# Earlier places for five VectorE and ScalarE operations around a block-attention stage

## The reference

```
h = h + moba_mixer(rmsnorm(h, norm_mix), w_qkv, q_gain, k_gain, w_o, rel_bias)
h = h + square(relu(rmsnorm(h, norm_ffn) @ w1)) @ w2

qkv = h @ w_qkv                          # q, k, v: 16 heads of 64
q, k = rmsnorm(q, q_gain), rmsnorm(k, k_gain)   # per head
p = softmax(q k^T / 8 + bias, causal)
o = (p v) @ w_o
```

## Time and profile before

| | us |
|---|---|
| median of 3 runs | 934.1 (933.73 to 934.14) |
| profiled execution, its own time | 932.37 |
| span of the profiled execution | 930.6 |
| DVE busy | 625.5 |
| ACT busy | 488.0 |

### The profile page before, as it was taken

One profiled execution on the slowest core, in us unless ns is written; L12 is line 12 of the kernel. 1 busy time (PEld: TensorE's weight loads), 2 busy tenths in 40 slices (PEclk: granted clock), 3 DMA queues, 4 the chain that ended last, 5 costly groups with the idle time before them and its releaser, 6 DMA issues.

```text
span 930.6 us, 13989 instructions
## 1 busy us (share of the span) xinstructions
PE 904.6 (97%) x5688; PEld 773.1 (83%) x5688; DVE 625.5 (67%) x1079; ACT 488.0 (52%) x732; POOL 38.3 (4%) x66
## 2 busy tenths in 40 slices
PE   9999999999999999988999999999998999999998
PEld 7987788887788887866999988878776799998886
DVE  5469978778888897775766654456677586665441
ACT  6545746646655855463655543346576365554330
POOL 2400010000000001000000000000000000000000
PEclk9999999999999999999999999999999999999999
DMA  8842363642245559550555565556463256655540
GB/s 298 301 145 91 99 202 115 225 135 91 92 148 169 180 200 271 153 146 15 167 183 182 194 207 187 184 179 207 155 204 113 91 181 188 192 196 195 183 157 23
DMA packets 79199, 154.58 MB, mean 166 GB/s; under 512 B 5543, under 2 KB 7879, under 8 KB 79136
## 3 DMA queue, kind: packets, MB, share of 16 engines
q1 hardware_dynamic: 75120, 142.81, 46.6%
q0 software_dynamic: 3872, 10.81, 4.7%
q10 hardware_dynamic: 144, 0.07, 0.0%
HBM read 152.57 MB, written 1.11 MB: 165 GB/s over the span
## 4 chain that ended last, share of the span: by engine, by line
PE 74%; DVE 14%; ACT 8%; issue 3%; DMA 0%; SPq 0%; DVEq 0%; ACTq 0%
PE ps L723 15%; PE ps L725 15%; PE ps L724 15%; PE ps L754 7%; PE ps L755 7%; PE ps L756 7%; DVE w_lo L1826 5%; ACT w_hi L1346 3%; PE ps L1028 1%; DVE area L2172 1%; DVE area L2308 1%; DVE area L2096 1%; ACT y_tok L1477 1%; PE ps_mid L1203 1%; ACT area L1564 1%
## 5 line engine op out<-in xcount | busy, mean ns | idle before, releaser
L1826 DVE TENSOR_TENSOR w_lo<-w_raw,w_hi 128x2048 fp32r<-128x2048 f32 (+1 forms) x134 | 302.3, 2261 | 187.1 <-ACT w_hi L1346 187.0
L1346 ACT ACTIVATE w_hi<-w_raw 128x2048 fp32r<-128x2048 f32 (+1 forms) x134 | 252.9, 1890 | 201.1 <-PE ps L725 147.2
L723 PE MATMUL ps<-w_hi,act_hi 128*128 128x512 f32 (+1 forms) x456 | 182.1, 399 | 2.2 <-ACT area L1364 1.0
L725 PE MATMUL ps<-w_hi,act_lo 128*128 128x512 f32 (+1 forms) x456 | 175.0, 384 | 0.0
L724 PE MATMUL ps<-w_lo,act_hi 128*128 128x512 f32 (+1 forms) x456 | 174.7, 383 | 0.0
L723 PE MATMUL ps<-w_hi,hid 128*128 128x512 f32 x296 | 116.1, 392 | 1.0 <-ACT area L1364 0.5
L725 PE MATMUL ps<-w_hi,hid 128*128 128x512 f32 x296 | 115.3, 389 | 0.0
L724 PE MATMUL ps<-w_lo,hid 128*128 128x512 f32 x296 | 115.2, 389 | 0.0
L754 PE MATMUL ps<-act_hi,w_hi 128*128 128x256 f32 x384 | 110.6, 288 | 0.4 <-DVE act_lo L2018 0.4
L755 PE MATMUL ps<-act_lo,w_hi 128*128 128x256 f32 x384 | 107.5, 280 | 0.0
L756 PE MATMUL ps<-act_hi,w_lo 128*128 128x256 f32 x384 | 107.5, 280 | 0.0
(11 more groups left out here) (356 smaller groups left out, 1231.5 us busy)
## 6 DMA issues: line engine op xcount, KB each, us to landing
w_raw<-in_ffn_w SPq DMA_DIRECT2D x64, 1024.0 KB, 5.3
w_raw<-in_w_in SPq DMA_DIRECT2D x22, 1024.0 KB, 5.5
w_raw<-in_a_w_qkv SPq DMA_DIRECT2D x18, 1024.0 KB, 5.0
w_raw<-in_b_w_qkv SPq DMA_DIRECT2D x12, 1024.0 KB, 5.1
w_raw<-in_w_out SPq DMA_DIRECT2D x8, 1024.0 KB, 5.0
w_raw<-in_b_w_o SPq DMA_DIRECT2D x4, 1024.0 KB, 5.0
w_raw<-in_w_in SPq DMA_DIRECT2D x8, 256.0 KB, 6.2
w_raw<-in_w_in SPq DMA_DIRECT2D x4, 512.0 KB, 3.5
```

The costliest lines, as they stand in the source:

```text
L723: pe.matmul(o, ah, wh, start=first, stop=False)
L725: mm = pe.matmul(o, al, wh, start=False, stop=last)
L1346: act.activation(w_hi[:, c % RING, :, 0:n], w_raw[:, c % RAW, :, 0:n], ACT.Copy).then_inc(w_hi_done, 1)
L1826: dve.tensor_tensor(lo, w_raw[:, c % RAW, :, 0:n], hi.bitcast(F), ALU.subtract).then_inc(w_lo_done, 1)
```

## The change

It moves five things. (1) The norms of heads 8 to 15 are done in two parts: heads 8 and 9 (`block_norms(f + 4, 0, 2)`) where all stood, and the other six in unit 5 behind the staging copy of pair 4; PE waits for the first part before pair 4 and for the second before pair 5. (2) In unit 7 DVE does the staging copy of pair 5 ahead of `scaled(8)` and `scaled(9)`. (3) ACT evicts half 0 of value block `f+5` in unit 8 ahead of the exponentials of units 10 and 11. (4) The split of the weight chunk at `f+6` goes from unit 14 to unit 12 on ACT and to unit 13 on DVE. (5) In `after_half` on DVE, half 0 of a residual block is evicted ahead of the weight split.

```diff
@@ stage_pair, PE
-                if p == 4:
-                    pe.wait_ge(qk_norm, 10)
+                if p in (4, 5):
+                    pe.wait_ge(qk_norm, 10 + 2 * (p - 4))
@@ block_attention, ACT
-                units(3, MOBA_HEADS, {..., 6: lambda: splits(f + 5, 0), 8: lambda: take(f + 5, 0), 9: lambda: splits(f + 5, 1),
-                                       14: lambda: splits(f + 6, 0)},
-                      front={1: lambda: take(f + 3, 1), 9: lambda: take(f + 5, 1)})
+                units(3, MOBA_HEADS, {..., 6: lambda: splits(f + 5, 0), 9: lambda: splits(f + 5, 1),
+                                       12: lambda: splits(f + 6, 0)},
+                      front={1: lambda: take(f + 3, 1), 8: lambda: take(f + 5, 0), 9: lambda: take(f + 5, 1)})
@@ block_norms, DVE
-            def block_norms(b):
+            def block_norms(b, h0=0, n=8):
                 for i in range(2):
-                    at = BLOCKS[b - 1 + i]["c0"]
-                    v = qkv[:, :, at:at + 512].rearrange("p t (h d) -> p t h d", d=HD)
-                    dve.tensor_tensor(v, v, spread(block_st[:, 6, 16 * i:16 * i + 1], [(8, 2), (1, 8), (0, HD)]), ALU.mult).then_inc(qk_norm, 1)
+                    at = BLOCKS[b - 1 + i]["c0"] + HD * h0
+                    v = qkv[:, :, at:at + HD * n].rearrange("p t (h d) -> p t h d", d=HD)
+                    dve.tensor_tensor(v, v, spread(block_st[:, 6, 16 * i + h0:16 * i + h0 + 1], [(8, 2), (1, n), (0, HD)]), ALU.mult).then_inc(qk_norm, 1)
@@ after_half, DVE
                     if also:
                         also()
+                    if BLOCKS[b]["use"] == "residual":
+                        take(b, 0)
                     splits(b, 0)
-                    take(b, 0)
+                    if BLOCKS[b]["use"] != "residual":
+                        take(b, 0)
@@ units, DVE
+                    if ph == 3 and u == 7:
+                        staged(BLOCK_STAGED[u])
                     if ph == 3 and u % 2 and u + 2 < n:
                         scaled(u + 1)
                         scaled(u + 2)
-                    if ph == 3 and u in BLOCK_STAGED:
+                    if ph == 3 and u in BLOCK_STAGED and u != 7:
                         staged(BLOCK_STAGED[u])
@@ block_attention, DVE
                 def hook4():
                     take(f + 4, 1)
-                    block_norms(f + 4)
+                    block_norms(f + 4, 0, 2)
+
+                def hook5():
+                    block_norms(f + 4, 2, 6)
+                    splits(f + 4, 1)
-                units(3, MOBA_HEADS, {..., 4: hook4, 5: lambda: splits(f + 4, 1), 7: ..., 10: ..., 14: lambda: splits(f + 6, 0)})
+                units(3, MOBA_HEADS, {..., 4: hook4, 5: hook5, 7: ..., 10: ..., 13: lambda: splits(f + 6, 0)})
```

More of the change, by code:

```diff
@@ L1629, in hook7 @@
                     splits(f + 4, 1)
-                units(3, MOBA_HEADS, {0: lambda: splits(f + 3, 0), 1: lambda: splits(f + 3, 1), 2: lambda: splits(f + 4, 0), 3: lambda: (take(f + 4, 0), take(f + 4, 1)), 5: lambda: splits(f + 4, 1), 6: lambda: splits(f + 5, 0), 8: lambda: take(f + 5, 0), 9: lambda: splits(f + 5, 1),
-                                       14: lambda: splits(f + 6, 0)},
-                      front={1: lambda: take(f + 3, 1), 9: lambda: take(f + 5, 1)})
+                units(3, MOBA_HEADS, {0: lambda: splits(f + 3, 0), 1: lambda: splits(f + 3, 1), 2: lambda: splits(f + 4, 0), 3: lambda: (take(f + 4, 0), take(f + 4, 1)), 5: lambda: splits(f + 4, 1), 6: lambda: splits(f + 5, 0), 9: lambda: splits(f + 5, 1),
+                                       12: lambda: splits(f + 6, 0)},
+                      front={1: lambda: take(f + 3, 1), 8: lambda: take(f + 5, 0), 9: lambda: take(f + 5, 1)})
                 pair_high(7)
@@ L2246, in hook4 @@
                     take(f + 4, 1)
-                    block_norms(f + 4)
-                units(3, MOBA_HEADS, {1: hook1, 2: lambda: splits(f + 3, 1), 3: lambda: splits(f + 4, 0), 4: hook4, 5: lambda: splits(f + 4, 1), 7: lambda: splits(f + 5, 0), 10: lambda: splits(f + 5, 1), 14: lambda: splits(f + 6, 0)})
+                    block_norms(f + 4, 0, 2)
+                def hook5():
+                    block_norms(f + 4, 2, 6)
+                    splits(f + 4, 1)
+                units(3, MOBA_HEADS, {1: hook1, 2: lambda: splits(f + 3, 1), 3: lambda: splits(f + 4, 0), 4: hook4, 5: hook5, 7: lambda: splits(f + 5, 0), 10: lambda: splits(f + 5, 1), 13: lambda: splits(f + 6, 0)})
                 pair_low(7)
```

## The result

| | before | changed |
|---|---|---|
| median of 4 runs each | 933.91 us | 926.24 us (925.13 to 927.26) |
| ratio, 95% interval | | 0.9925 (0.9907 to 0.9943) |
| profiled execution, own time | 932.37 us | 926.48 us |
| span | 930.6 us | 924.7 us |

The forecast was faster, at 928.7 us with a range from 927.1. Three of the four runs of the kernel before are the ones behind the 934.1 us that the forecast started from.

A forecast was written before the change was run, and what follows sets the result against it. PE was taken to bound the kernel, so only its idle time could be gained: 0.75 + 3.17 + 1.47 = 5.39 us, moving the median from 934.1 to 928.7 us, with a range of 927.1 to 931.0.

The forecast's parts named there:

- Sum: Gains of 0.75 us at moba's entry, 3.17 to pair 4's output and 1.47 at pair 7's output: 5.39 us.
- Entry: At the start of moba, evicting residual half 0 before DVE's weight split removes PE's idle time: 0.75 us.
- Up to the output of pair 4: Mixer lead from norms, staging copy and value eviction together, after a new wait there: 3.17 us.
- Last: Before pair 7's output, PE no longer waits for DVE's copy of unit 15 behind a weight split: 1.47 us.
- lower bound's 4.2 us: Smallest gain: new wait at pair 4 a whole microsecond, first norms at the page's full price; 929.9 us.
- The base: Profiled execution lies 1.7 us under the median, so its forecast 927.0 us becomes a median of 928.7, from 934.1.
- Norms, staging copy: Before pair 4's transposes PE gains 1.60 us, DVE 1.27; before pair 5's scores PE gains 1.53 more.
- Value eviction: At mobao's first step 0.52 us gained, mostly handed back in a 0.45 us wait before pair 4's output.
- Weight split: Split of unit 14 moved into DVE's idle time; pair 6's low part about 1.5 us later, unnoticed; gain 1.47 us.
- second wait: Units 7 to 9: ACT's late half delays pair 5's copy, divisions and split; gain 3.9 us, 930.2; chance 0.15.
- FFN that takes the gain back: Next FFN's start hangs on weight stream or load; mixer's 4.64 us lost, 0.75 left: 933.4 us; chance 0.05.
- lower clock in the mixer: Denser PE work drops TensorE's granted clock to 1.2 GHz; 10 us of it gives 938.7 us; chance 0.02.

The follow-up runs named there:

- e2: Kernel before with only the residual half 0 eviction moved ahead of the weight split; 931.18 us, ratio 0.9991.
- e3: Changed kernel without the residual half 0 eviction ahead of the weight split; 927.75 us, ratio 0.9959.
- e5: Changed kernel with the norms of heads 8 to 15 whole again; 929.01 us in its only execution, a profiled one.
- e6: Changed kernel with DVE's staging copy of pair 5 back behind the divisions of units 8 and 9; 930.18 us in its only execution, a profiled one.
- e11: Changed kernel with DVE's staging copy of pair 5 back behind the divisions of units 8 and 9, run again; median 929.13 us.
- e4: Changed kernel with ACT's eviction of value half 0 back behind the exponentials; median 929.35 us.
- e7: Changed kernel with the weight split back in unit 14; 927.39 us in its only execution, a profiled one.
- e8: Changed kernel with ACT's eviction of value half 1 moved between the exponentials of units 10 and 11; median 927.09 us, ratio 0.9931.
- e12: Same kernel as e8, value half 1 evicted between the exponentials of units 10 and 11; 925.34 us in its only execution, a profiled one.

## Why the prediction was wrong, point by point

- **Sum.** 5.39 us were forecast against the profiled execution; it gained 5.89 (932.37 to 926.48), of which 0.2 us was there before the first place of the change. Entry: 0.75 forecast, 1.05 measured (e2; 1.08 in e3). The step was the choice of idle time over start-to-start distance; the modelled end of the last matmul hides part of a wait, and the first matmul behind a wait is longer. Up to the output of pair 4: 3.17 forecast, 3.02 measured. Last: 1.47 forecast, 1.56 measured. The lower bound's 4.2 us does not follow from its own terms: the wait at a whole microsecond and the full price of the norms make about 4.7.
- **The base: the step that failed.** "It lies 1.7 us under the median, so the median goes from 934.1 to 928.7." The three runs behind 934.1 lay at the upper end of what this kernel does: 42 further runs have medians of 931.54, 932.61 and 932.22 on their three chips. A median of three at its upper end was thus taken for the kernel's time, and the gain of one execution was set against it, while the new time was drawn from the changed kernel's middle. Of the 2.5 us between 928.7 and 926.24 this step is 1.7; the gain of 5.9 instead of 5.4 is 0.5, and the last 0.2 is the distance of the new median from its own profiled execution. Had I set the gain of 5.4 against the profiled execution's 932.37, the forecast would have been 927.0, and 926.24 well within a range as wide. The range took the spread of the three runs, 0.4 us; 930.05 to 936.08 is that of the 42. Why those three lay high isn't known: neither their clocks nor their chip are recorded.
- **Norms, staging copy.** Right in mechanism and size. DVE carried on 1.27 us as forecast (1.26, e5), PE started the scores of pair 5 without a wait. What I did not see is what the old wait can do besides: with the others in, it is 1.9 us long, and in both profiles that have it (e6, e11) the lower clock followed, which makes part 2 worth 2.6 us there.
- **Value eviction.** The new wait before the output of pair 4 came as forecast in place and cause, at 0.9 us instead of 0.45: PE reached mobao 0.3 us earlier than the idle times said, and the output started 0.15 us later. "This part is worth next to nothing, and what it gives is handed back one piece later" was wrong: 1.4 us (e4). I took the part's worth from the wait of the kernel before, 0.52 us, and did not ask how long that wait would be with the other parts in: 2.11 us. The prediction's own numbers had the answer. Without part 3 ACT's chain, 1.60 us earlier, starts mobao at 715.46 - 1.60 = 713.86 and the output at 717.05 - 1.60 = 715.45, against 713.88 with it: 1.57 us. The sum was not touched, since it took the 3.17 us with all parts in.
- **Weight split.** Right: 1.54 us (e7). Pair 6's low part came later and nobody waited.
- **The fixed cost of small operations.** The norms cost by their pitch, the distance from one start to the next: 0.67 us for the first two and 1.74 for the others, 2.41 against 2.27 in one piece. That is 0.14 us more, as priced, and not the 0.31 that the formula for one operation's duration on the page "VectorE: DVE Perf Modes" of the Trainium skill, section "The TRN2 errata", gives when it is charged in full each time.
- **Rivals.** No second wait, no FFN that takes the gain back, and no lower clock in the mixer in the changed kernel's three profiles.

## What to carry to other kernels

Set a gain that was summed from one execution against that same execution, and ask for the spread of many runs, on more than one chip, before a median of three becomes the base. The worth of one part is found with all other parts in: the wait that would stand there (here four times the one in the old trace), less the wait that comes up behind it. Where two waits have work between them, an earlier end of the first lets that work run ahead of the second. Behind a wait of TensorE of some 2 us look at the granted clock: of the three profiles with such a wait here, two lost 1.5 us to it and one nothing.

## What the hardware showed that was not expected

- In the two profiles without part 2, the granted clock went to its lower level right behind a wait of 1.87 us, and cost 1.5 us; behind the 2.11 us of e4's profile it stayed at 1.00. Single executions differ by such stretches elsewhere. On one chip the median of the kernel before is 1.0 us (931.34 to 932.32) or 1.6 us (930.84 to 932.41) higher at a mean clock of 0.998 than at 1.000.
- The second up product ran at 11.31 us a block in the profiles of e2 (one) and of e8 and e12 (one kernel, two), and at 11.20 in the eleven others, at a clock of 1.00 and with PE busy throughout, though none of these edits touches that product. The first FFN's up product ran at 11.20 in the same three profiles. The unprofiled runs speak against a loss in every execution of these kernels: e2's nine at 0.998 gain the full 1.2 us, and e8's two at 1.000 (924.64 and 924.56) are 7.5 us under the kernel before on their chip (932.09), where e12's profiled one is 6.0 under (925.34 and 931.34). I have no cause for it, and none was tried.
